# First attention tile: GpSimd splits six of eight output-weight blocks and the values' low part

## The reference, cut to what matters

```python
attn = bidir_block_attention(q, k, v)            # softmax(q k^T / 8) v
lru = (h_fwd + h_bwd) * gelu(y_lru)
merged = concat([rms_norm(attn, attn_out_g), rms_norm(lru, lru_out_g)])
mix = merged @ w_out                             # [1024] x [1024, 1024]
h = layer_norm(alpha * h + mix)                  # then the router and the experts
```

## Time and profile before

| | us |
|---|---|
| median of 3 runs | 1604.24 (1603.88 to 1604.75) |
| the profiled execution | 1599.9 |
| its span, first to last instruction | 1598.1 |
| PE busy | 1444.6 (90%) |
| DVE busy | 1126.0 (70%) |
| ACT busy | 928.1 (58%) |
| POOL busy | 481.1 (30%) |

### The profile page before, as it was taken

One profiled execution on the slowest core, in us unless ns is written; L12 is line 12 of the kernel. 1 busy time (PEld: TensorE's weight loads), 2 busy tenths in 40 slices (PEclk: granted clock), 3 DMA queues, 4 the chain that ended last, 5 costly groups with the idle time before them and its releaser, 6 DMA issues. The chain is left out here.

```text
span 1598.1 us, 30295 instructions
## 1 busy us (share of the span) xinstructions
PE 1444.6 (90%) x8945; PEld 1258.7 (79%) x8947; DVE 1126.0 (70%) x2198; ACT 928.1 (58%) x1624; POOL 481.1 (30%) x347
## 2 busy tenths in 40 slices
PE   6999989999996999999999999975899999999940
PEld 5999977777765899999999999963777788777820
DVE  8787547999977888888888888877444334444237
ACT  4444338788776666666666666633565445555325
POOL 1212124565440011111121111131454433555318
PEclk9999999999998999999999999996999999999965
DMA  8865641544454112111112121127798787786576
GB/s 290 297 229 195 231 144 70 192 165 151 166 174 163 52 61 79 60 59 59 61 67 92 65 73 60 47 96 239 230 277 251 205 246 189 216 266 151 110 228 256
DMA packets 126214, 250.09 MB, mean 156 GB/s; under 512 B 24498, under 2 KB 77746, under 8 KB 126132
## 3 DMA queue, kind: packets, MB, share of 16 engines
q1 hardware_dynamic: 94000, 160.97, 29.2%
q0 software_dynamic: 12528, 45.99, 12.3%
q10 hardware_dynamic: 19604, 42.09, 7.0%
HBM read 154.35 MB, written 94.67 MB: 156 GB/s over the span
## 5 line engine op out<-in xcount | busy, mean ns | idle before, releaser
L1755 DVE TENSOR_TENSOR d_probs_t_lo<-d_pt_ps,d_probs_t_hi 128x512 fp32r<-128x512 f32 x256 | 165.0, 686 | 63.6 <-ACT d_probs_t_hi L1669 62.0
L1669 ACT ACTIVATE d_probs_t_hi<-d_pt_ps 128x512 fp32r<-128x512 f32 x256 | 139.2, 596 | 95.6 <-PE d_pt_ps L1550 89.3
L1731 DVE TENSOR_REDUCE d_neg_max<-d_s_ps 128x1 f32<-128x1024 f32 x128 | 155.5, 1215 | 3.4 <-PE d_s_ps L1539 3.4
L122 PE MATMUL acc<-k_hi,wl_hi 128*128 128x256 f32 x512 | 145.8, 285 | 4.4 <-DVE k_lo L597 4.4
L1652 ACT ACTIVATE d_probs<-d_s_ps,d_neg_max 128x1024 f32<-128x1024 f32 x128 | 143.4, 1121 | 4.3 <-DVE d_neg_max L1731 4.3
L122 PE MATMUL e_a_ps<-up_hi,e_xt_hi 128*128 x336 | 137.1, 408 | 9.7 <-DVE e_xt_lo L2591 5.0
L123 PE MATMUL acc<-k_lo,wl_hi 128*128 128x256 f32 x512 | 144.9, 283 | 0.0
L124 PE MATMUL acc<-k_hi,wl_lo 128*128 128x256 f32 x512 | 144.9, 283 | 0.0
L1550 PE MATMUL d_pt_ps<-ident,d_probs 128*128 128x128 f32 x1024 | 132.9, 273 | 4.7 <-ACT d_probs L1652 3.2
L1564 PE MATMUL d_ot_ps<-d_probs_t_hi,d_v_split 128*128 128x256 f32 x512 | 127.4, 287 | 8.3 <-DVE d_probs_t_lo L1755 8.3
L123 PE MATMUL e_a_ps<-up_lo,e_xt_hi 128*128 x336 | 133.4, 397 | 0.0
(11 more groups left out here) (414 smaller groups left out, 4089.3 us busy)
## 6 DMA issues: line engine op xcount, KB each, us to landing
up_raw<-in_exp_w SPq DMA_DIRECT2D x32, 1024.0 KB, 9.5
down_raw<-in_exp_w SPq DMA_DIRECT2D x16, 1024.0 KB, 14.1
d_h_tile<-h_dram SPq DMA_DIRECT2D x16, 522.0 KB, 4.8
h_dram<-v_all ACTq DMA_DIRECT2D x16, 512.0 KB, 3.2
ht_hi_dram<-k_hi ACTq DMA_DIRECT2D x8, 1024.0 KB, 4.3
ht_lo_dram<-k_lo ACTq DMA_DIRECT2D x8, 1024.0 KB, 6.7
d_q_tile<-q_dram SPq DMA_DIRECT2D x16, 512.0 KB, 4.3
h_dram<-l_h_tile SPq DMA_DIRECT2D x16, 512.0 KB
```

The costliest lines, as they stand in the source:

```text
L122: pe.matmul(out, lhs[0], rhs[0], start=first, stop=False)
L1669: act.activation(pt_hi[:, c * HALF:(c + 1) * HALF, h % 2], pt_ps[c][:], ACT.Copy).then_inc(pth_done[c], 1)
L1731: dve.tensor_reduce(nm[:, u, h:h + 1], s_ps[h % 2][:], AX, ALU.max, negate=True).then_inc(nm_done, 1)
L1755: dve.tensor_tensor(pt_lo[:, part, h % 2], pt_ps[c][:], pt_hi[:, part, h % 2].bitcast(F32), ALU.subtract)\
```

## The change

Six of the eight blocks of `w_out`, in the order 6, 7, 0, 1, 2, 3, are split by GpSimd alone: a tensor_scalar by the gain into the high part, a tensor_scalar by the gain in place, and a subtraction into the low part, each waiting for the one before. They have three load buffers in turn (the two of before and a new one). Blocks 4 and 5 stay with ACT and DVE, in heads 2 and 5, with a load buffer of their own. GpSimd first makes the low part of the values. TensorE waits before the second tile for the two kept blocks and GpSimd's first two, and in the second tile's head 3 for all six of GpSimd. On DVE, the router's gained columns and the start of the recurrent norms (the reduction, the scaling and the three guess steps) move to head 3, the router's split (ACT and DVE) and the row sums' copies to head 4, the nine Newton steps to head 6.

```diff
@@ -1389,7 +1389,10 @@
         stats = sb("stats1", [P, 12])
         shift1 = sb("shift1", [P, 1])
         s_t = [sb("s_tile0", [P, DW]), s_last]
-        raw = [s_t[1][:, 0:D], h1[:]]
+        ON_POOL = [6, 7, 0, 1, 2, 3]
+        BY_HEAD = {2: 4, 5: 5}
+        raw_beside = sb("wo_raw", [P, D])
+        raw = [s_t[1][:, 0:D], h1[:], sb("wo_raw_pool", [P, D])[:]]
         s_ps = [ps(f"s_ps{j}", [P, SEQ]) for j in range(2)]
         pt_ps = [ps(f"pt_ps{c}", [P, HALF, P]) for c in range(2)]
         ot_ps = ps("ot_ps", [P, 512])
@@ -1400,7 +1403,10 @@
 
         rows_in = sem("rows_loaded_d")
         out_g_in = sem("out_g_loaded")
-        raw_in = [sem(f"wo_raw_loaded{j}") for j in range(2)]
+        raw_in = [sem(f"wo_raw_loaded{j}") for j in range(len(raw))]
+        beside_in = sem("wo_raw_beside_loaded")
+        pool_gained = sem("wo_on_pool_gained")
+        pool_lo_made = sem("wo_lo_made_on_pool")
         ones_made = sem("ones_made")
         vh_made = sem("v_hi_made")
         vl_made = sem("v_lo_made")
@@ -1476,6 +1482,14 @@
             def load_y(t):
                 sp.dma_start(yt[:], lru_dram[:, :, bass.ds(t * P, P)].rearrange("f p t -> p f t")).then_inc(y_in, 16)
 
+            def load_for_pool(i):
+                rows = slice(ON_POOL[i] * P, (ON_POOL[i] + 1) * P)
+                sp.dma_start(raw[i % 3], w_out[0, rows, :]).then_inc(raw_in[i % 3], 16)
+
+            def load_beside(h):
+                rows = slice(BY_HEAD[h] * P, (BY_HEAD[h] + 1) * P)
+                sp.dma_start(raw_beside[:], w_out[0, rows, :]).then_inc(beside_in, 16)
+
             def store_h1(t):
                 sp.wait_ge(h1_done, 2 * t + 2)
                 for dst in (h1_dram, sum_dram):
@@ -1487,17 +1501,22 @@
             with nc.allow_non_contiguous_dma("small per-feature vectors and router columns"):
                 sp.dma_start(out_g[:, 0:FT], attn_g[0].rearrange("(f p) -> p f", p=P)).then_inc(out_g_in, 16)
                 sp.dma_start(out_g[:, FT:KD], lru_g[0].rearrange("(f p) -> p f", p=P)).then_inc(out_g_in, 16)
-                for k in range(2):
-                    sp.dma_start(raw[k], w_out[0, k * P:(k + 1) * P, :]).then_inc(raw_in[k], 16)
+                for i in range(len(raw)):
+                    load_for_pool(i)
+                load_beside(2)
                 load_y(0)
             sp.dma_start(rb_b[:, 0:G], row(router_bg[0], G)).then_inc(rows_in, 16)
             sp.dma_start(rb_b[:, G:RW], row(router_be[0].rearrange("g e -> (g e)"), NE)).then_inc(rows_in, 16)
             sp.dma_start(g_b[:], row(ln_g[0], D)).then_inc(rows_in, 16)
             sp.dma_start(b_b[:], row(ln_b[0], D)).then_inc(rows_in, 16)
             load_h(0)
-            for k in range(2, KD):
-                sp.wait_ge(lo_made, k - 1)
-                sp.dma_start(raw[k % 2], w_out[0, k * P:(k + 1) * P, :]).then_inc(raw_in[k % 2], 16)
+            sp.wait_ge(pool_lo_made, 1)
+            load_for_pool(3)
+            sp.wait_ge(lo_made, 1)
+            load_beside(5)
+            for i in (4, 5):
+                sp.wait_ge(pool_lo_made, i - 2)
+                load_for_pool(i)
             sp.wait_ge(yl_done, 1)
             load_y(1)
 
@@ -1611,8 +1630,9 @@
                 if h == 0:
                     if not late:
                         pe.wait_ge(rows_read, 2)
-                        pe.wait_ge(lo_made, KD)
+                        pe.wait_ge(lo_made, 2)
                         pe.wait_ge(rl_made, 1)
+                        pe.wait_ge(pool_lo_made, 2)
                     pe.wait_ge(yl_done, t)
                     project(FT, 0)
                 if h == 1:
@@ -1621,6 +1641,8 @@
                     turn_o()
                 if h in (2, 4):
                     project(FT, h // 2)
+                if h == 3 and not late:
+                    pe.wait_ge(pool_lo_made, 6)
                 if h in (3, 5, 6):
                     project(0, (3, 5, 6).index(h))
 
@@ -1669,14 +1691,14 @@
                     act.activation(pt_hi[:, c * HALF:(c + 1) * HALF, h % 2], pt_ps[c][:], ACT.Copy).then_inc(pth_done[c], 1)
                 if nxt[0]:
                     exp(*nxt[0])
-                if not post:
-
-                    act.wait_ge(raw_in[h % 2], 16 * (h // 2 + 1))
+                if not post and h in BY_HEAD:
+                    k = BY_HEAD[h]
+                    act.wait_ge(beside_in, 16 * (list(BY_HEAD).index(h) + 1))
                     act.wait_ge(out_g_in, 32)
-                    act.activation(w_hi[:, h, 0:D], raw[h % 2], ACT.Copy, scale=out_g[:, h:h + 1]).then_inc(hi_made, 1)
-                    if h == 1:
-                        act.wait_ge(wg_made, 1)
-                        act.activation(w_hi[:, :, D:], w_rg[:], ACT.Copy).then_inc(rh_made, 1)
+                    act.activation(w_hi[:, k, 0:D], raw_beside[:], ACT.Copy, scale=out_g[:, k:k + 1]).then_inc(hi_made, 1)
+                if not post and h == 4:
+                    act.wait_ge(wg_made, 1)
+                    act.activation(w_hi[:, :, D:], w_rg[:], ACT.Copy).then_inc(rh_made, 1)
                 beside()
 
             def norm_pair(t, i):
@@ -1730,22 +1752,17 @@
                 dve.wait_ge(s_done, n + 1)
                 dve.tensor_reduce(nm[:, u, h:h + 1], s_ps[h % 2][:], AX, ALU.max, negate=True).then_inc(nm_done, 1)
 
-            def lru_norms():
-                link = Chain(dve, dve_link)
-                link(dve.tensor_reduce(lru_tmp[:].rearrange("p (s c) -> p s c", s=SEQS),
-                                       lru_sums[:].rearrange("p (s f) c -> p s c f", s=SEQS), AX, ALU.add))
-                link(dve.tensor_scalar(lru_var[:], lru_tmp[:], ALPHA ** 2 / LW, LN_EPS * ALPHA ** 2, ALU.mult, ALU.add))
-                rsqrt(dve, link, lru_var[:], rl[:], lru_tmp[:], wide=True)
+            lru_link = Chain(dve, dve_link)
+
+            def lru_norms_start():
+                lru_link(dve.tensor_reduce(lru_tmp[:].rearrange("p (s c) -> p s c", s=SEQS),
+                                           lru_sums[:].rearrange("p (s f) c -> p s c f", s=SEQS), AX, ALU.add))
+                lru_link(dve.tensor_scalar(lru_var[:], lru_tmp[:], ALPHA ** 2 / LW, LN_EPS * ALPHA ** 2, ALU.mult, ALU.add))
+                rsqrt_guess(dve, lru_link, lru_var[:], rl[:], lru_tmp[:])
 
             def first():
-                lru_norms()
                 neg_max(0, 0, 0)
                 neg_max(0, 0, 1)
-                dve.wait_ge(vh_made, 1)
-                dve.wait_ge(out_g_in, 32)
-                dve.tensor_tensor(w_rg[:], w_r[:], out_g[:].unsqueeze(2).broadcast_to([P, KD, RW]), ALU.mult).then_inc(wg_made, 1)
-                dve.tensor_tensor(vs[:, :, :, 1], v_all[:].rearrange("p t (g d) -> p t g d", g=NKV),
-                                  vs[:, :, :, 0].bitcast(F32), ALU.subtract).then_inc(vl_made, 1)
 
             def head(t, u, s, h, nxt, post, beside):
                 n = NQ * t + h
@@ -1757,13 +1774,21 @@
                 if nxt[1]:
                     neg_max(*nxt[1])
                 if not post:
-                    dve.wait_ge(hi_made, h + 1)
-                    dve.scalar_tensor_tensor(w_lo[:, h, 0:D], raw[h % 2], out_g[:, h:h + 1], w_hi[:, h, 0:D].bitcast(F32),
-                                             ALU.mult, ALU.subtract).then_inc(lo_made, 1)
-                    if h == 1:
+                    if h in BY_HEAD:
+                        k = BY_HEAD[h]
+                        dve.wait_ge(hi_made, list(BY_HEAD).index(h) + 1)
+                        dve.scalar_tensor_tensor(w_lo[:, k, 0:D], raw_beside[:], out_g[:, k:k + 1], w_hi[:, k, 0:D].bitcast(F32),
+                                                 ALU.mult, ALU.subtract).then_inc(lo_made, 1)
+                    if h == 3:
+                        dve.wait_ge(out_g_in, 32)
+                        dve.tensor_tensor(w_rg[:], w_r[:], out_g[:].unsqueeze(2).broadcast_to([P, KD, RW]), ALU.mult).then_inc(wg_made, 1)
+                        lru_norms_start()
+                    if h == 4:
                         dve.wait_ge(rh_made, 1)
                         dve.tensor_tensor(w_lo[:, :, D:], w_rg[:], w_hi[:, :, D:].bitcast(F32), ALU.subtract).then_inc(rl_made, 1)
-                    if h == 2:
+                    if h == 6:
+                        rsqrt_steps(dve, lru_link, lru_var[:], rl[:], lru_tmp[:], wide=True)
+                    if h == 4:
                         dve.wait_ge(rows_done, 1)
                         dve.wait_ge(rows_in, 64)
                         dve.tensor_copy(r_rows[:, 0], m_ps[:, 0:RW]).then_inc(rows_read, 1)
@@ -1930,6 +1955,21 @@
                     pool.wait_ge(hg_done, 2 * t + half + 3)
                     pool.tensor_tensor(h1[:, part], h1[:, part], b_b[:, part], ALU.add).then_inc(h1_done, 1)
 
+            def split_w(i):
+                k, part = ON_POOL[i], raw[i % 3]
+                pool.wait_ge(raw_in[i % 3], 16 * (i // 3 + 1))
```

(12 more changed lines are left out.)

## The result

The changed kernel is slower: the ratio of its time to the time before is 1.0025, with a 95% interval of 1.0013 to 1.0037, from 20 runs of each (medians 1607.06 and 1603.97 us). That ratio is 4.0 us, 2.1 to 5.9 (the two medians are 3.1 us apart). The profiled execution is a long one, 1611.1 us. The time from the router's first step to the end, which no kernel here alters, was 522.7 us in the profile before, 528.1 in this one, 526.4 in a second profile of the same kernel (e8), and anything from 521.9 to 528.2 in the others.

The account below looks back on a forecast made before the run. First attention tile bound by hand-over between engines, later tiles by TensorE. Free GpSimd work gives -1.2 us; with DVE held up, replays give +7.0 or +3.9, middle +5.5: 1604.2 + 5.5 = 1609.7 us, range 1602.8 to 1614.

Parts of the forecast that it names:

- the replay with whole holds: First tile: DVE's small steps wait out each GpSimd instruction, one step per instruction; head 9's exponential 537.15 against 530.17, +7.0 us.
- the other one: First-tile replay where a second DVE step slips in at each GpSimd wait; head 3's chain ends at 516.2, +3.9 us.
- pair 4: First tile, head 7's to head 9's exponential: w_out block leaves (1.40), nine norm steps come in (1.89); 8.84 us.
- Pairs 1 and 2: First tile's first two pairs of heads: 0.56 us less in the first; the second 8.72, with w_lo held 0.35 us.
- Pair 1's term: First tile's first pair: v's low part leaves DVE, so the transposes start 0.56 us earlier.
- GpSimd's length: GpSimd's tensor_scalar of 1024 taken as 1.25 us, a block 5.0 us, six blocks ending about 522 undisturbed.
- The hold: First tile: GpSimd's instructions hold DVE's small or two-SBUF-operand steps, one step per instruction; PSUM readers are spared.
- free GpSimd work: First tile if GpSimd's work holds up nothing: third pair 7.40 us, sum of the four pairs -1.2 us.
- Head 6: First tile: nine chained norm steps ahead of PV's low part, 0.21 us apart, 1.89 us, running free after GpSimd is done.
- The rival of a slow GpSimd: First tile: tensor_scalar takes 2.35 us, block 7.3, GpSimd lasts until 538 and hits head 6; +15 us, 1619; chance 10%.
- Covered by some 20 us: Second tile's head 3: GpSimd's six blocks end about 522, PE needs them at 542.34, so no wait.
- The norms gained nothing by leaving the start: Start of attention: moving the norms away saves nothing, since DVE did them while PE waited for the first q tile.

Follow-up runs that it names:

- e8: The changed kernel profiled once more, unaltered; pairs 8.48, 8.36, 8.14, 14.19 us, router's first step 588.3 us from the first exponential (changed 588.4).
- e11: Kernel before, with only the values' low part moved to GpSimd; head 9's exponential 36.7 us from the first (before 37.3), router's first step 582.5 (before 582.5).
- e4: Changed kernel plus a probe ahead of the first tile: DVE's chained small steps beside one block's GpSimd instructions; head 9's exponential at 43.8 us (changed 42.1).
- e3: Kernel before, with only the recurrent norms' steps moved to heads 3 and 6, GpSimd idle; last pair 10.34 us instead of 8.35.
- e9: Changed kernel plus 16 unread matmuls between head 7's scores and PV, second run of that kernel; last pair 11.87 us instead of 14.19.
- e1: Changed kernel with the recurrent norms whole again at the start on VectorE; last pair 7.12 us, third tile's first exponential 72.5 us (changed 73.6).
- e5: Changed kernel with GpSimd's two tensor_scalar per block replaced by a broadcast multiply and a copy; block 5.4 us, head 9's exponential 44.4 us (changed 42.1).
- e2: Changed kernel plus 16 unread matmuls in head 7's gap, first run, with late clock; inconclusive, pairs 8.95, 11.75, 8.05, 10.42 us.

## Why the prediction held, and where it did not

The sign and size held: +5.5 us forecast, +4.0 measured (2.1 to 5.9), and in the profile head 9's exponential 4.8 us late. The way there was partly another, and that the size held is in part luck, since two errors cancelled: pair 3 came out 7.1 us shorter than in the replay with whole holds (8.15 against 15.2; 3.7 shorter than in the other one, 11.9), pair 4 5.4 us longer (14.19 against 8.84).

- **Pairs 1 and 2.** Predicted 8.55 and 8.72 (8.37 without a hold), measured 8.49 and 8.35. Pair 1's term was right, and e11 shows it alone. In pair 2 w_lo was not held (1.28 us at 506.51), which fits e4: GpSimd was already past the first third of a tensor_scalar (504.68 to 507.53).
- **GpSimd's length** was the mis-sized term: I took 1.25 us for a tensor_scalar, between bounds of 0.9 and 2.35. It took 2.85, outside both. The only tensor_scalar in the trace, 64 elements in 0.40 us, was long for its width; 2.85 less 0.40 over 960 elements is 2.6 ns each, three times the memset's slope that I used. The upper bound should not have been the two-input form. The Trainium skill's line that one-input work runs roughly at line rate (GPSIMD Engine Reference, section "Engine selection") agrees with the copy, 1.04 us, and not with the tensor_scalar.
- **The hold** was right in kind and wrong in extent. The rule I had from the earlier trace rows, one chained step per GpSimd instruction for its whole length, came from two-input GpSimd work and holds for that (2.30 us at 524.20). A tensor_scalar lets steps through for a third or two of its time (e4). So head 3's chain took 2.7 us, not 8.5, and pair 3 was 8.15, not 15. (It was not the 7.40 of free GpSimd work either: with its two held steps the chain ended at 513.09 and the next transposes waited 0.87 us for DVE.) The Trainium skill's exclusive lock for the whole instruction (SBUF — State Buffer, section "SBUF: two separate sides") agrees with the subtraction and not with the tensor_scalar.
- **Head 6** I had put behind GpSimd's end and priced at 1.9 us. With GpSimd lasting to 542.9, two of the nine steps were held, 3.0 us more. e3 confirms the 1.9 (2.0) of the place alone. The rival of a slow GpSimd had this mechanism, and with it whole holds and +15 us; the short holds of the tensor_scalar kept it from that.
- **The clock** was not in the sum at all. PE's 4.9 us without work brought the granted clock to half, and PV and what followed took 2.3 us longer (e9). The 14.19 us of pair 4 are thus 7.1 as in e1, 2.0 for the chain's place (e3), 3.0 held and 2.3 for the clock: 14.4, a sum of terms from different kernels.
- **"Covered by some 20 us"** was wrong: the cover was 4.3 us, and gone in e1, where PE waits 4.2 us for GpSimd's last block and again loses the clock.
- The norms gained nothing by leaving the start, as predicted: e1 puts them back, and from PE's first scores to the first exponential it takes 3.4 us as in the changed kernel.

## What to carry to other kernels

Before work is moved to an idle engine, price its instructions by a row of the same kind and width; if there is none, measure the one instruction first, since every cover (the time left before something waits for it) and every hold hangs on it. What an idle engine holds up in a neighbour depends on what each reads: move GpSimd's work beside VectorE's PSUM readers, and keep VectorE's chains of small SBUF steps (here worth 0.2 us each) out of it and off the path to TensorE. When a fix gains far less two stages on than where it was made, look there for a second wait that the first had hidden. And before two profiles are compared, compare their first microseconds: here the profiles in which the clock rose late had other steps held.

## What the runs showed of the hardware

- GpSimd, 128x1024 float32: tensor_scalar 2.85 us by a column, 2.77 by a constant; multiply by the same column, broadcast as a second input, 1.89; subtraction of two tensors 2.35; copy 1.04.
- A GpSimd tensor_scalar held VectorE's two-input steps for its first 0.95 to 1.1 us only, and one-input steps of 16 columns for its first and last 0.9 to 1.0; a two-input GpSimd instruction held both for its whole length. Where VectorE's longer instruction came first, GpSimd's lasted longer instead (2.88 us for 1.89 in e5).
- VectorE's instructions that read PSUM ran at their usual length beside GpSimd all through (low parts 1.29 us for two).
- The granted clock was at 0.50 behind a gap of 4.9 us of PE (changed kernel), one of 4.2 us (e1) and one of 3.6 us (e5). It stayed at 1.00 behind one of 3.4 us (e3), but fell in the course of PV behind gaps of 3.3 us (e2, pair 2), 2.2 us (e4, pair 2) and 1.9 us (e5, pair 4). So the length of the last gap alone does not tell whether it falls. These three, and the 3.6 us, are in profiles with the late clock at the start.
- The first tile's stretch from PV to the next odd exponential took 3.6 to 3.7 us at full clock, and 5.0 to 6.0 us where the clock was at half for a part of it.
